# The context half of ab_in's first chunks computed ahead of the norm, and modulation units 16 to 31 taken off TensorE, with the second vector's products on ScalarE and GpSimd

## The reference

```python
cond_x = silu(c)                 # vector 0: for x
cond_c = silu(c_ctx)             # vector 1: for the context
for i in range(2):
    sx1, cx1, gx1, sx2, cx2, gx2 = split(cond_x @ ada_w[i] + ada_b[i], 6)
    sc1, cc1, gc1, sc2, cc2, gc2 = split(cond_c @ ada_w[i] + ada_b[i], 6)
    hx = rms(x, norm_mix_g[i]) * (1 + cx1) + sx1
    if i == 0:
        x = x + gx1 * conv_fourier_mixer(hx, ab_w_in, ab_conv_w, ab_w_out)
        hc = rms(ctx, norm_mix_g[i]) * (1 + cc1) + sc1
        ctx = ctx + gc1 * conv_fourier_mixer(hc, ab_w_in, ab_conv_w, ab_w_out)
    else:
        ...                      # neighbourhood attention, context as keys and values
    x = x + gx2 * mlp(rms(x, norm_mlp_g[i]) * (1 + cx2) + sx2)
    ...                          # the same for ctx, not in the last layer
```

## Time and profile before

| | us |
|---|---|
| median of three runs | 1307.44 |
| lowest and highest | 1306.98, 1308.37 |
| span of the profiled execution | 1306.1 |
| TensorE busy in it | 1289.2 |
| VectorE, ScalarE, GpSimd busy | 871.6, 594.9, 427.6 |

### The profile page before, as it was taken

How to read it: one execution, slowest core, us unless ns; L and a number is a source line. 1 busy time by engine, 2 the same in 40 slices (tenths; PEclk the granted TensorE clock), 3 DMA queues, 4 the chain that set the end, 5 groups by cost and what they waited for, 6 DMA issues and landing times.

```text
span 1306.1 us, 19845 instructions
## 1 busy us (share of the span) xinstructions
PE 1289.2 (99%) x7748; PEld 1098.8 (84%) x7748; DVE 871.6 (67%) x1303; ACT 594.9 (46%) x955; POOL 427.6 (33%) x433
## 2 busy tenths in 40 slices
...
DMA packets 66269, 219.97 MB, mean 168 GB/s; under 512 B 9121, under 2 KB 12449, under 8 KB 66177
## 3 DMA queue, kind: packets, MB, share of 16 engines
...
HBM read 217.21 MB, written 1.05 MB: 167 GB/s over the span
## 4 chain that ended last, share of the span: by engine, by line
PE 77%; DVE 12%; issue 4%; DMA 3%; ACT 3%; SPq 0%; POOL 0%; DVEq 0%; ACTq 0%; POOLq 0%
PE ps L628 19%; PE ps L642 18%; PE ps L640 18%; PE ps L618 8%; DVE wlo L1717 4%; PE ps L620 4%; DVE tmp L2007 2%; DMA raw<-in_w_in 2%; PE ps L1078 1%; DVE Y L1744 1%; PE ps L1105 1%; PE ps L1092 1%; ACT A L1262 1%; PE ps L743 1%; PE ps L1071 1%
## 5 line engine op out<-in xcount | busy, mean ns | idle before, releaser
L628 PE MATMUL ps<-A,whi 128*128 128x256 f32 (+2 forms) x1564 | 511.8, 327 | 0.0
L642 PE MATMUL ps<-A,wlo 128*128 128x256 f32 (+2 forms) x1536 | 491.1, 320 | 2.0 <-DVE wlo L1717 2.0
L640 PE MATMUL ps<-A,whi 128*128 128x256 f32 (+2 forms) x1536 | 490.5, 319 | 0.2 <-DVE A L1730 0.2
L1717 DVE TENSOR_TENSOR wlo<-raw,whi 128x1024 fp32r<-128x1024 f32 (+1 forms) x302 | 396.8, 1317 | 85.7 <-ACT whi L1237 85.3
L1237 ACT ACTIVATE whi<-raw 128x1024 fp32r<-128x1024 f32 (+1 forms) x302 | 316.7, 1051 | 265.4 <-PE ps L642 137.5
L628 PEld LDWEIGHTS ps<-A,whi 128*128 128x128 f32 x1564 | 296.6, 190 | 42.6 <-issue 18.7
L642 PEld LDWEIGHTS ps<-A,wlo 128*128 128x128 f32 x1536 | 291.3, 190 | 24.0 <-DVE wlo L1717 2.8
L640 PEld LDWEIGHTS ps<-A,whi 128*128 128x128 f32 x1536 | 291.8, 190 | 22.0 <-issue 1.7
L2398 POOL TENSOR_TENSOR H<-tmp,H 128x256 fp32r<-128x256 f32 (+1 forms) x86 | 125.6, 1461 | 56.9 <-ACT H L1552 43.3
L618 PE MATMUL ps<-H,whi 128*128 128x512 f32 x400 | 140.4, 396 | 0.2 <-POOL H L2398 0.2
L620 PE MATMUL ps<-H,wlo 128*128 128x256 f32 x400 | 111.7, 279 | 0.5 <-DVE wlo L1717 0.4
...
## 6 DMA issues: line engine op xcount, KB each, us to landing
...
```

Of the source, the lines that this page charges most:

```text
L628: e.matmul(o, w_hi, ah, start=k == 0, stop=False)
L640: e.matmul(o, w_hi, al, start=False, stop=False)
L642: m = e.matmul(o, w_lo, ah, start=False, stop=last)
L1717: e.tensor_tensor(wlo[i % NRAW][:, :cols], raw[i % NRAW][:, :cols], plain(whi[s % NHI][:, :cols]), SUB).then_inc(S("wlo").sem, 1)
```

## The change

Three things change together.

1. **Units 16 to 31 (quad 1) leave TensorE.** Eight of them leave w_in and the eight ahead of ab_in go. They are now in `MOD`: five in w_down (after units 1 to 5), eleven in ab_in. The other units in `MOD` move later: quad 2 is cut into its even pair (summed in ab_out) and its odd pair (units in w1_0a, summed there into bank 3), and `SUMS` lists seven sums instead of six.
2. **For 24 units (`SHARED`: quad 1 and the even pair of quad 2) VectorE does vector 0 only.** ScalarE multiplies the unit by vector 1 (`ada_place` in the scalar program) into a product tile, or into `modsum` for the first unit of a pair, and GpSimd adds the product tile to `modsum` (`ada_place` in the gpsimd program), 21 times. In w_down there is one product tile, `down_product`; later there are two. A load that follows such a unit in the ring waits for both VectorE and ScalarE.
3. **ab_in's first chunks are taken apart.** `context(n, ks)` does the RIGHT half of chunks 0 and 1 (all three products) as soon as the column sums are issued; three of chunk 0's blocks stand between the two pairs of sums. `three_chunks` then does the LEFT halves of both with the high part, chunk 2 with the high part, and the low passes of all three. The scaled chunks have a tile each (`n2_x`) instead of five in turn, and the weight splits of w_down's last unit and of ab_in's first units are made earlier.

```diff
@@ -45,23 +45,37 @@
-ADA_BEFORE = {"ab_in": 8, "w1_0a": 6, "na_in": 8}
-AHEAD = {"ab_in": 4, "w1_0a": 3, "na_in": 3}
+ADA_BEFORE = {"w1_0a": 6, "na_in": 8}
+AHEAD = {"w1_0a": 3, "na_in": 3}
-ADA_AFTER = {"w_in": (6, 24)}
-MOD = [*range(32, 48), *range(54, 88)]
+ADA_AFTER = {"w_in": (6, 16)}
+MOD = [*range(16, 32), *range(32, 48, 2), *range(33, 48, 2), *range(54, 64, 2), *range(55, 64, 2), *range(64, 88)]
+FIRST = {16, 17, 32, 33, 54, 55, 64, 65, 80, 81}
+SHARED = [*range(16, 32), *range(32, 48, 2)]
+SHARED_AT = {n: x for x, n in enumerate(SHARED)}
+ADDS = {n: sum(m not in FIRST for m in SHARED[:x + 1]) for n, x in SHARED_AT.items()}
-MOD_AFTER = {"w_down": (1, 3), "ab_in": (5, 6, 7, 9, 10, 12, 13, 14), "ab_out": range(6), "w1_0a": (*EVEN, 5, 11),
-             "w2_0a": EVEN, "w1_0b": EVEN, "w2_0b": EVEN}
-MOD_SUMMED = {("ab_out", 6): 2, ("w1_0a", 15): 3, ("w1_0b", 15): 4, ("na_in", 0): 5}
-ADA_WRITTEN = {("w_in", 34): 0, ("ab_in", 2): 1, ("ab_out", 7): 2, ("w2_0a", 1): 3, ("w2_0b", 1): 4, ("na_in", 4): 5}
+MOD_AFTER = {"w_down": (1, 2, 3, 4, 5), "ab_in": range(4, 16), "ab_out": (0, 1, 1, 2, 3, 4, 5), "w1_0a": (1, 2, 4, 5, 7, 8, 10, 11),
+             "w2_0a": (0, 2, 3, 5, 6, 8, 9, 11, 12, 14), "w1_0b": range(2, 16), "w2_0b": (0, 1, *range(5, 13))}
+SUMS = [(0, None), (1, None), (2, 0), (2, 1), (3, None), (4, None), (5, None)]
+MOD_SUMMED = {("ab_out", -1): 1, ("ab_out", 6): 2, ("w1_0a", 13): 3, ("w1_0b", 0): 4, ("w2_0b", 1): 5, ("na_in", 0): 6}
+ADA_WRITTEN = {("w_in", 34): 0, ("ab_out", 0): 1, ("ab_out", 7): 2, ("w1_0a", 15): 3, ("w1_0b", 1): 4, ("w2_0b", 2): 5, ("na_in", 4): 6}
+def units_of(x):
+    quad, pair = SUMS[x]
+    return [n for n in MOD if n // 16 == quad and pair in (None, n % 2)]
...
@@ -171,7 +185,7 @@
-        behind = 0 if PLAN[i] == ("na_out", 0) or e + 1 < len(TAKEN) and any(TAKEN[e + 1] == FRONT[x][0] for x in AHEAD) else 1
+        behind = 0 if PLAN[i] in (("na_out", 0), ("w_down", 21), ("ab_in", 0)) or e + 1 < len(TAKEN) and any(TAKEN[e + 1] == FRONT[x][0] for x in AHEAD) else 1
...
+    first_modsum = [[sb("modsum_x", 1024, at=h_at + 53248), modsum[1][1]], [modsum[1][0], sb("modsum_y", 1024, at=h_at + 49152)]]
+    down_product = h32("down_product", 1024, 45056)
+    mod_product = [h32(f"mod_product{i}", 1024, 4096 * i) for i in range(2)]
+    def product_tile(n):
+        x = SHARED_AT[n]
+        return down_product if x < len(MOD_AFTER["w_down"]) else mod_product[x % 2]
+    def product_before(n):
+        x = SHARED_AT[n]
+        return [m for m in SHARED[:x] if m not in FIRST and product_tile(m) is product_tile(n)][-1:]
...
@@ -513,7 +546,10 @@
-                w.wait_ge(S("mod"), MOD_AT[PLAN[i - NRAW][1]] + 1)
+                n = PLAN[i - NRAW][1]
+                w.wait_ge(S("mod"), MOD_AT[n] + 1)
+                if n in SHARED:
+                    w.wait_ge(S("mod_x"), SHARED_AT[n] + 1)
...
@@ -966,16 +1014,70 @@
+        def n2_hi(k):
+            w.wait_ge(S("nc_hi"), k + 1)
+            w.wait_ge(S("n2_hi"), k + 1)
+        def n2_lo(k):
+            w.wait_ge(S("nc_lo"), k + 1)
+            w.wait_ge(S("n2_lo"), k + 1)
+        def context(n, ks):
+            s, o = SPLIT_AT["ab_in", n], bank_of("ab_in", n)[:, RIGHT]
+            bank_free("ab_in", n)
+            w.wait_ge(S("whi"), s + 1)
+            low_ready(s)
+            for k in ks:
+                w_hi = whi[s % NHI][:, 128 * k:128 * k + 128]
+                w_lo = wlo[SPLIT[s] % NRAW][:, 128 * k:128 * k + 128]
+                w.wait_ge(S("nc_hi"), k + 1)
+                e.matmul(o, w_hi, Ahi[:, k, RIGHT], start=k == 0, stop=False)
+                e.matmul(o, w_lo, Ahi[:, k, RIGHT], start=False, stop=False)
+                w.wait_ge(S("nc_lo"), k + 1)
+                e.matmul(o, w_hi, Alo[:, k, RIGHT], start=False, stop=k == 7)
+        def three_chunks():
+            def weights(n, k):
+                s = SPLIT_AT["ab_in", n]
+                c = slice(128 * k, 128 * k + 128)
+                return whi[s % NHI][:, c], wlo[SPLIT[s] % NRAW][:, c]
+            for k in range(8):
+                n2_hi(k)
+                for n in range(2):
+                    w_hi, w_lo = weights(n, k)
+                    o = bank_of("ab_in", n)[:, LEFT]
+                    e.matmul(o, w_hi, Ahi[:, k, LEFT], start=k == 0, stop=False)
+                    e.matmul(o, w_lo, Ahi[:, k, LEFT], start=False, stop=False)
+            s, o = SPLIT_AT["ab_in", 2], bank_of("ab_in", 2)
+            bank_free("ab_in", 2)
+            w.wait_ge(S("whi"), s + 1)
+            low_ready(s)
+            for k in range(8):
+                w_hi, w_lo = weights(2, k)
+                e.matmul(o, w_hi, Ahi[:, k], start=k == 0, stop=False)
+                e.matmul(o, w_lo, Ahi[:, k], start=False, stop=False)
+            for n, cols in ((0, LEFT), (1, LEFT), (2, WHOLE)):
+                for k in range(8):
+                    n2_lo(k)
+                    m = e.matmul(bank_of("ab_in", n)[:, cols], weights(n, k)[0], Alo[:, k, cols], start=False, stop=k == 7)
+                m.then_inc(S("mm").sem, 1)
-        ada_before("ab_in", 0, 2)
+        context(0, range(3))
+        context(0, range(3, 8))
+        context(1, range(8))
+        three_chunks()
@@ -992,18 +1094,9 @@
-            written("ab_in", n)
-        def n2_hi(k):
-            w.wait_ge(S("nc_hi"), k + 1)
-            w.wait_ge(S("n2_hi"), k + 1)
-        def n2_lo(k):
-            w.wait_ge(S("nc_lo"), k + 1)
-            w.wait_ge(S("n2_lo"), k + 1)
-        ada_before("ab_in", 2)
-        linear("ab_in", 512, lambda k: (Ahi[:, k], Alo[:, k]), n2_hi, n2_lo, during=during_ab)
+        for n in range(3):
+            during_ab(n)
+        linear("ab_in", 512, lambda k: (Ahi[:, k], Alo[:, k]), n2_hi, n2_lo, during=during_ab, begin=3)
...
@@ -1243,6 +1339,25 @@
+        def ada_place(i):
+            his(i)
+            n = PLAN[i][1]
+            if n not in SHARED:
+                return
+            quad, k, pair = n // 16, n // 2 % 8, n % 2
+            w.wait_ge(S(f"load{i % NRAW}"), 16 * (i // NRAW + 1))
+            if n in FIRST:
+                w.wait_ge(S("up_conv"), 44)
+                into = mod_tile(quad, pair, 1)
+            else:
+                if product_tile(n) is not down_product:
+                    w.wait_ge(S("ab_f"), 4)
+                for m in product_before(n):
+                    w.wait_ge(S("mod_p"), ADDS[m])
+                into = product_tile(n)
+            e.activation(into, raw[i % NRAW], ACT.Copy, scale=cond[:, k, 1:2]).then_inc(S("mod_x").sem, 1)
...
@@ -1491,17 +1605,14 @@
-            e.activation(Ahi[:, c, LEFT], tmp[c % 5][:, :256], ACT.Identity, bias=ada[:, 0, 0, c:c + 1]).then_inc(S("n2_hi").sem, 1)
-        his(UNIT["w_down", 21])
-        for i in before("ab_in"):
-            his(i)
+            e.activation(Ahi[:, c, LEFT], n2_x[c], ACT.Identity, bias=ada[:, 0, 0, c:c + 1]).then_inc(S("n2_hi").sem, 1)
-                his(i)
+                ada_place(i)
...
@@ -2080,20 +2192,14 @@
-            e.scalar_tensor_tensor(Alo[:, c, LEFT], tmp[c % 5][:, :256], ada[:, 0, 0, c:c + 1], plain(Ahi[:, c, LEFT]),
+            e.scalar_tensor_tensor(Alo[:, c, LEFT], n2_x[c], ada[:, 0, 0, c:c + 1], plain(Ahi[:, c, LEFT]),
-            if c >= 5:
-                w.wait_ge(S("n2_lo"), c - 4)
-            e.scalar_tensor_tensor(tmp[c % 5][:, :256], R[:, c, LEFT], GF[:, c:c + 1], r12, MUL, MUL).then_inc(S("n2_t").sem, 1)
-            if c >= 4:
-                n2_lo(c - 4)
-        for c in range(4, 8):
+            e.scalar_tensor_tensor(n2_x[c], R[:, c, LEFT], GF[:, c:c + 1], r12, MUL, MUL).then_inc(S("n2_t").sem, 1)
+        for c in range(8):
-        for i in before("ab_in"):
-            ada_place(i)
...
@@ -2494,7 +2603,19 @@
+        def ada_place(i):
+            n = PLAN[i][1]
+            if n in SHARED and n not in FIRST:
+                total = mod_tile(n // 16, n % 2, 1)
+                w.wait_ge(S("mod_x"), SHARED_AT[n] + 1)
+                w.wait_ge(S("mod_p"), ADDS[n - 2])
+                e.tensor_tensor(total, total, product_tile(n), ADD).then_inc(S("mod_p").sem, 1)
+        for what, i in walk("w_down"):
+            if what == "ada":
+                ada_place(i)
@@ -2502,10 +2623,17 @@
+        for what, i in walk("ab_in"):
+            if what == "ada":
+                ada_place(i)
-        parts("m0", ssum, lambda c: sq[c % 2])
+        for what, i in walk("ab_out"):
+            if what == "chunk" and i >= 2:
+                part("m0", ssum, sq[(i - 1) % 2], i - 1)
+            if what == "ada":
+                ada_place(i)
```

More of the change, by code:

```diff
@@ L118, in weight_plan @@
                 modulation(4, here)
-            owed += u in MOD_AFTER.get(name, ())
+            owed += sum(x == u for x in MOD_AFTER.get(name, ()))
             if ahead and u == 1:
@@ L427, in half @@
         return slice(256 * q, 256 * q + 256)
+    n2_x = [tmp[c // 2][:, half(c % 2)] for c in range(8)]
     def rows_of(h):
@@ L735, in ada_unit @@
```

(2 more changed lines are left out.)

129 lines of the change are left out of this document (74 added, 55 removed).

## The result

The changed kernel takes 1318.24 us (median of 4 runs, 1316.57 to 1319.73) against 1307.24 of the kernel before on the same chip: 1.0079 of it, 95% interval 1.0067 to 1.0092. It is slower by 11 us; forecast were 5 us less. A second measurement on another chip gave 1.0065 (1.0047 to 1.0084). The profiled execution took 1317.43 us, with a span of 1315.6, 9.5 more than before. On other chips the kernel before had medians of 1309.45, 1307.92 and 1309.51, so experiments are compared by their ratio to it and by their stages.

A forecast was written before the change was run, and what follows sets the result against it. The prediction took TensorE's issued work as the bound (busy 1289.2 of 1306.1 us). Terms -3.1 + 1.5 - 6.3 + 2.6 = -5.3 us gave a span of 1300.8, carried to 1302.2 us; 8-in-10 range 1297.8 to 1307.8.

The forecast's parts named there:

- step 5: ab_in, ab_out and the stretch from 640 to 905 us: the remaining vector work and additions stay hidden, at no cost.
- step 2: w_down: five units instead of two, a serial chain through one product tile makes TensorE wait, +1.5 us.
- step 4: Ahead of and after ab_out, and in w1_0a: TensorE must sum quad 1 and do two more transpose groups, +2.6 us.
- Step 1: w_in: eight units leave TensorE, the first group's gain is mostly lost to a GpSimd wait, -3.1 us.
- my ends of -0.4 and +5.6: Limits of the w_down term: all of it hidden, -0.4 us, or GpSimd additions of 4.9 us each, +5.6 us.
- Step 3: Front of ab_in: units and transposes leave and gaps close, so chunk 3 starts sooner after w_down, -6.3 us.
- Its end of -6.8: Limit of the term for ab_in's front, if the folds cost their second 0.89 us elsewhere: -6.8 us.
- rival C: w_down and ab_out: GpSimd's 128x1024 addition is the bound, at 4.9 us each +6.1, 1313.5 us; chance 0.08.
- The sign that I named for a wrong forecast: ab_out: TensorE waiting for GpSimd or for the modulation's sums would show the forecast wrong; no size given.

The follow-up runs named there:

- e11: The changed kernel measured again with no edit, on another chip: 1.0065 of the kernel before, 1318.27 us.
- e3: The changed kernel with nothing shared, VectorE making both vectors of every unit: 0.9985 of the kernel before, 1307.76 us.
- e2: The changed kernel with second vectors shared in ab_out only, VectorE making both for quad 1: 1.0012 of the kernel before, 1310.88 us.
- e4: e3 with units 16 to 19 back on TensorE in w_in, two units in w_down and 11 in ab_in: 0.9957 of the kernel before, 1304.3 us.
- e1: The changed kernel with each GpSimd addition cut to 32 columns instead of 1024, all else left: 0.9964 of the kernel before, 1305.16 us.

## Why the prediction was wrong

The main fault is step 5, "the rest is hidden": I priced it at nothing because VectorE has 12 vector operations in ab_in instead of 16, and counted operations only, not the time in which GpSimd shuts it out. With step 2's error and the extra in step 4 it turns -5.3 into +9.5.

- **Step 1, w_in, -3.1.** Right in mechanism: measured -3.6, the first head's transposes start at 109.95 instead of 110.73 behind a wait of 0.94 us for GpSimd, and the wait of 119.29 is gone. The five kernels with the first group back reach w_up's sum at 198.65 to 201.14, so that group was worth anything between 0.1 and 2.6 us; the runs don't settle it.
- **Step 2, w_down, +1.5.** Measured +4.2 (+3.5 in e11), between my ends of -0.4 and +5.6. The loop of products through one tile came as described: ScalarE waited 4.65 us for an addition, and TensorE then 1.25 us at 351.67 and 0.67 at 355.39 for low parts. With small additions these two go, and w_down is 1.55 us shorter (0.9 against e11). e3, where VectorE does both vectors, has no loop and is no shorter. The rest, 2.6 us, is the context sum's wait, which I put at 0.3 to 0.5 us and which is 2.28. My own rows already gave more: three products of 1.05 less the 1.72 of waiting shown put the last square at 345.3, not 344.4, and the gap at about 1.1. What I left out is the transfers: among the squares ScalarE waited for w_down's weights, 1.04 us in the changed kernel and over 3 in e2 and e3, and not at all in e4. That the loads of the added units cause this is likely, but no run changes them alone.
- **Step 3, the front, -6.3.** Right: -6.5 in every kernel without a gap, chunk 3 at 20.4 us instead of the 20.6 forecast. (Its end of -6.8 is a slip: -6.3 and 0.89 more are -7.2.)
- **Step 4, +2.6.** Too low by about 1.3. e1, with no wait in ab_out, has +1.7 there and +2.2 from w1_0a on, 3.9 in sum. What the further 1.3 us are stays open.
- **Step 5, 0.** ab_in costs +8.0 against the kernels without a gap (101.08 to 93.04; +6.9 in e11), ab_out +3.95 against e1 (65.54 to 61.59): a gap of 2.4 us ahead of quad 2's sum and some 1.5 us at the slower pace in and behind it.
- **The price of an addition** was near: I took 2.7 us, and the 21 additions have a mean of 2.9, from 2.4 alone to 3.4 beside VectorE and once 4.13. So rival C's condition (4.3 us or more) never held. The sign that I named for a wrong forecast, a wait for GpSimd in ab_out, appeared all the same. GpSimd's total there was as forecast (30.65 us of 45, against 29), but the last addition could not start before the last product, which came 1.5 us ahead of TensorE's need. An addition that takes 2.4 us alone is too long for that; from the rows above I estimate 1.5 us of the gap without VectorE's interference and 0.9 with it on top. Why the transfer ahead of that product came late is not shown.
- **The rule that was cited**, from the Trainium skill (SBUF — State Buffer, "Who interferes with whom"), stood in step 2 for 2 us and was not carried to step 5. It is the mechanism: the row at 457.90 agrees within 0.2 us with a lock for the whole instruction. The Trainium skill says it as advice too (Perfetto Trace Analysis, "Optimizing Scalar/DVE Operations"): offloading between GpSimd and VectorE might not help. e1 and e3 agree: ab_in is 8.0 us shorter without the additions.
- **The clock.** I took 2.4 GHz behind every new gap; two of them, at 480 and at 543, brought a stretch at the lower level, 1.2 GHz, which no term had.

With -3.6 (step 1), +4.2 (step 2), -6.5 (step 3), +3.9 (step 4), +8.0 and +3.95 (step 5), and -0.4 for the rest of the rows, the sum is +9.5.
